# Selected attention by groups of heads: eight heads of the first token block at once, four of the second

## The reference, cut to what matters

```
q_chunk = (start + arange(128)) // 64                 # one block of 128 queries
admissible = key_chunk[None, :] <= q_chunk[:, None]
score = sum_h w[t,h] * relu(q_idx[t,h] . k_idx[s])    # the indexer
top_val, top_idx = top_k(where(admissible, score, -inf), 128)
logits = einsum('bqhd,bqkhd->bhqk', q, k[top_idx]) * 64 ** -0.5
p = softmax(where(valid, logits, -inf))
out = einsum('bhqk,bqkhd->bqhd', p, v[top_idx])
```

## Time and profile before

| what | us |
|---|---|
| median of three runs | 2717.39 |
| lowest and highest | 2716.45, 2717.55 |
| profiled execution, its own time | 2718.07 |
| its span | 2716.8 |
| TensorE busy in it | 2677.7 (99%) |
| VectorE busy | 1219.1 (45%) |
| ScalarE busy | 1049.5 (39%) |
| GpSimd busy | 1139.0 (42%) |

### The profile page before, as it was taken

One profiled execution on the slowest core, in us unless ns is written; L12 is line 12 of the kernel. 1 busy time (PEld: TensorE's weight loads), 2 busy tenths in 40 slices (PEclk: granted clock), 3 DMA queues, 4 the chain that ended last, 5 costly groups with the idle time before them and its releaser, 6 DMA issues.

```text
span 2716.8 us, 36054 instructions
## 1 busy us (share of the span) xinstructions
PE 2677.7 (99%) x13721; PEld 2153.6 (79%) x13721; DVE 1219.1 (45%) x2468; ACT 1049.5 (39%) x2005; POOL 1139.0 (42%) x894
## 2 busy tenths in 40 slices
PE   8999999999999999999999999999999999999998
PEld 6888888897778877776788888887777678888887
DVE  4434334443555456544246424265644423642426
ACT  3333434443446343452333424234445333342422
POOL 4434344435342443333365444444333336444443
PEclk9999999999999999999999999999999999999999
DMA  6444343432331332224252333324222425233331
GB/s 191 130 116 124 98 125 97 130 125 86 109 94 55 112 97 78 78 82 134 100 182 72 116 93 95 99 79 130 81 68 88 136 93 175 83 118 100 93 93 63
DMA packets 215056, 286.39 MB, mean 105 GB/s; under 512 B 16862, under 2 KB 154562, under 8 KB 214116
## 3 DMA queue, kind: packets, MB, share of 16 engines
q1 hardware_dynamic: 214884, 284.08, 34.2%
HBM read 248.31 MB, written 18.94 MB: 98 GB/s over the span
## 4 chain that ended last, share of the span: by engine, by line
PE 96%; DVE 2%; ACT 1%; POOL 1%; issue 1%; DMA 0%; ACTq 0%; DVEq 0%; POOLq 0%
PE banks L1687 39%; PE banks L1684 29%; PE banks L1680 13%; PE banks L1818 2%; PE banks L1705 2%; PE banks L1744 1%; PE banks L1800 1%; PE banks L1904 1%; PE banks L1720 1%; PE banks L1927 1%; PE banks L1839 1%; PE banks L1977 1%; PE banks L1861 1%; PE banks L1890 1%; PE banks L1786 1%; PE banks L1915 1%
## 5 line engine op out<-in xcount | busy, mean ns | idle before, releaser
L2991 POOL TENSOR_TENSOR WS<-WR,WS 128x512 fp32r<-128x512 f32 (+2 forms) x676 | 856.3, 1300 | 1048.6 <-ACT WS L2040 1048.6
L1687 PE MATMUL banks<-WS,UT 128*128 128x512 f32 (+1 forms) x3696 | 797.0, 365 | 3.9 <-DVE UT L2393 3.9
L1687 PEld LDWEIGHTS banks<-WS,UT 128*128 128x128 f32 x3696 | 605.8, 190 | 131.4 <-issue 36.4
L1684 PE MATMUL banks<-UT,WS 128*128 128x512 f32 (+1 forms) x2832 | 660.8, 392 | 0.7 <-ACT AR L2222 0.7
L1684 PEld LDWEIGHTS banks<-UT,WS 128*128 128x128 f32 (+1 forms) x2832 | 526.0, 187 | 125.8 <-issue 16.0
L2040 ACT ACTIVATE WS<-WR 128x1024 fp32r<-128x1024 f32 (+1 forms) x344 | 333.1, 1018 | 221.4 <-PE banks L1687 144.3
L1680 PE MATMUL banks<-UT,WS 128*128 128x512 f32 x1536 | 371.1, 395 | 0.0
L1680 PEld LDWEIGHTS banks<-UT,WS 128*128 128x128 f32 x1536 | 282.5, 188 | 61.9 <-issue 4.9
L1687 PE MATMUL banks<-WS,AT 128*128 128x512 f32 x1296 | 308.5, 396 | 0.0
L1687 PEld LDWEIGHTS banks<-WS,AT 128*128 128x128 f32 x1296 | 242.4, 188 | 58.2 <-ACT WS L2040 0.7
L2989 POOL TENSOR_TENSOR WS<-WR,WS 128x512 fp32r<-128x512 f32 x128 | 177.9, 1422 | 251.6 <-ACT WS L2036 251.6
(11 more groups left out here) (226 smaller groups left out, 2665.2 us busy)
## 6 DMA issues: line engine op xcount, KB each, us to landing
WR<-in_w_in SPq DMA_DIRECT2D x112, 512.0 KB, 3.6
WR<-in_w_up SPq DMA_DIRECT2D x88, 512.0 KB, 3.5
WR<-in_dil_w_in SPq DMA_DIRECT2D x64, 512.0 KB, 3.8
WR<-in_w_down SPq DMA_DIRECT2D x40, 512.0 KB, 3.7
WR<-in_diff_w_in SPq DMA_DIRECT2D x32, 512.0 KB, 3.8
WR<-in_dil_w_in SPq DMA_DIRECT2D x32, 256.0 KB, 3.2
AR<-AF SPq DMA_DIRECT2D x128, 64.0 KB, 2.3
AR<-AF SPq DMA_DIRECT2D x64, 128.0 KB, 2.4
```

What stands on the lines that cost most here:

```text
L1684: mm = pe.matmul(B[bank][0:c, :], w[part][:, kk, g * P:g * P + c], act[:, other, kk, :], start=start, stop=stop)
L1687: mm = pe.matmul(B[bank][:, off:off + n], act[:, other, before_k + kk, g * P:g * P + P], w[part][:, kk, :], start=start, stop=stop)
L2991: ge.tensor_tensor(slot(i, 1)[:, s], raw(i)[:, s], slot(i, 0)[:, s].bitcast(F32), ALU.subtract).then_inc(lo_p.sem, 1)
```

## The change

The 32 units are grouped. `att_groups()` lists (first unit, m), with m pairs of heads in each group: one group of 4 pairs for block 0, two groups of 2 pairs for block 1, and single pairs for blocks 2 and 3. One `scores3` step multiplies all m pairs, side by side in banks 4 and 5 (m w columns in each). There are two `turn3` steps, one for each half of the group's heads, each with m (b + 1) transposes into one bank and one copy by ScalarE. One `out3` makes the sums of all m pairs in one bank with one copy by VectorE. The reciprocals are taken m at a time. Each step yields as many turns as the single steps that it takes the place of: m for scores (one more for the first), m for each turn, m for the sums. Small values get places of their own, as there are now eight of each.

```diff
+def att_groups():
+    return [(0, 4), (8, 2), (12, 2)] + [(n, 1) for n in range(16, 32, 2)]
...
-                if n % 2 == 0:
-                    self.step("scores3", l, n)
+                self.step("scores3", l, n, m)
+                for _ in range(m + (n == 0)):
                     yield
-                    if n == 0:
-                        yield
-
-            def turn(n):
-                self.step("turn3", l, n)
-                yield
-
-            def out_of(n):
-                if n % 2:
-                    self.step("out3", l, n)
+
+            def turn(n, m, half):
+                self.step("turn3", l, n, m, half)
+                for _ in range(m):
                     yield
 
-            yield from self.staged(len(units), [scores, turn, out_of])
+            def out_of(n, m):
+                self.step("out3", l, n, m)
+                for _ in range(m):
+                    yield
+
+            for g in range(len(groups) + 1):
+                if g > 0:
+                    yield from turn(*groups[g - 1], 1)
+                if g < len(groups):
+                    yield from scores(*groups[g])
+                if g > 0:
+                    yield from out_of(*groups[g - 1])
+                if g < len(groups):
+                    yield from turn(*groups[g], 0)
...
# tensor()
-                    for e in range(2):
-                        r = 64 * e
-                        mm = pe.matmul(B[4 + e][:, 0:w], aqT[r:r + 64, h // 2, b * P:b * P + P],
-                                       akT[r:r + 64, h // 2, 0:w], start=True, stop=True)
+                    for q in range(m):
+                        for e in range(2):
+                            r = slice(64 * e, 64 * e + 64)
+                            mm = pe.matmul(B[4 + e][:, q * w:q * w + w], aqT[r, h // 2 + q, b * P:b * P + P],
+                                           akT[r, h // 2 + q, 0:w], start=True, stop=True)
                     mm.then_inc(scored.sem, 1)
...
-                    pe.wait_ge(weights_scaled.sem, weights_scaled.at["3", l, n])
+                    e = n + half * m + m - 1
+                    pe.wait_ge(weights_scaled.sem, weights_scaled.at["3", l, e])
...
-                    for j in range(b + 1):
-                        mm = pe.transpose(B[k][:, j * P:j * P + P], arr(o_p + 512 * e + j * P, P), IDN)
+                    for j in range(m * (b + 1)):
+                        o = o_p + 512 * half + P * j
+                        mm = pe.transpose(B[k][:, j * P:j * P + P], arr(o, P), IDN)
...
-                    for j in range(b + 1):
-                        for e in range(2):
-                            o = (h - 1 + e) * 64
-                            mm = pe.matmul(B[ob][64 * e:64 * e + 64, 0:P], av[:, j, o:o + 64],
-                                           arr(o_pt + 512 * e + j * P, P), start=(j == 0), stop=(j == b))
+                    for q in range(m):
+                        for j in range(b + 1):
+                            for e in range(2):
+                                o = (h + 2 * q + e) * 64
+                                pt = o_pt + 512 // m * (2 * q + e) + j * P
+                                mm = pe.matmul(B[ob][64 * e:64 * e + 64, P * q:P * q + P], av[:, j, o:o + 64],
+                                               arr(pt, P), start=(j == 0), stop=(j == b))
...
# scalar(), scores3 and turn3
+                    for e in range(2 * m):
+                        v = arr(o_p + 512 // m * e, w)
                         se.wait_ge(maxed.sem, maxed.at["3", l, n + e])
-                        if n >= 2:
-                            se.wait_ge(weights_scaled.sem, weights_scaled.at["3", l, n + e - 2])
+                        if e == 0 and n > 0:
+                            se.wait_ge(weights_scaled.sem, weights_scaled.at["3", l, n - 1])
...
+                    w = P * (sel_units[n][0] + 1) * m
+                    se.wait_ge(pturned.sem, pturned.at["3", l, n, half])
...
# vector(), scores3
+                    for e in range(2 * m):
+                        if n > 0 and 512 // m * e % 512 == 0:
+                            ve.wait_ge(pturned.sem, pturned.at["3", l, g, e // m])
+                        o = e // 2 * w
+                        ve.tensor_tensor_reduce(arr(o_p + 512 // m * e, w), B[4 + e % 2][:, o:o + w],
                                                 SEL[b] if b else CT[:, C_KM:C_KM + P], -0.125, -GONE, ALU.add,
-                                                ALU.min, SM[:, MX + e:MX + e + 1]).then_inc(maxed.sem, 1)
+                                                ALU.min, SM[:, MX3 + e:MX3 + e + 1]).then_inc(maxed.sem, 1)
+                    for half in range(2):
+                        z = slice(m * half, m * half + m)
+                        ve.wait_ge(exped.sem, exped.at["3", l, n + z.stop - 1])
+                        ve.reciprocal(SM[:, RZ3 + z.start:RZ3 + z.stop],
+                                      SM[:, ZS3 + z.start:ZS3 + z.stop]).then_inc(recip.sem, 1)
+                        ve.wait_ge(recip.sem, recip.at["3", l, n, half])
+                        for e in range(m * half, m * half + m):
+                            v = arr(o_p + 512 // m * e, w)
+                            ve.tensor_scalar(v, v, SM[:, RZ3 + e:RZ3 + e + 1], None,
+                                             ALU.mult).then_inc(weights_scaled.sem, 1)
...
# vector(), out3
-                    ve.tensor_copy(XA[:, h // 2, b * P:b * P + P],
-                                   B[bank6["out", "3", l, n]][:, 0:P]).then_inc(out_copied.sem, 1)
+                    ve.tensor_copy(XA[:, h // 2:h // 2 + m, b * P:b * P + P],
+                                   B[bank6["out", "3", l, n]][:, 0:P * m].rearrange("p (q t) -> p q t", q=m)
+                                   ).then_inc(out_copied.sem, 1)
```

More of the change, by code:

```diff
@@ L972, in build @@
         E32, QT, SUB, LJ = 344, 384, 512, 640
+        MX3, ZS3, RZ3 = 640, 648, 656
         oSIN, oCOS = 17088, 17120
@@ L1270, in build @@
                 key = (kind[-1], *a)
+                if kind == "turn3":
+                    l, n, m, half = a
+                    key = ("3", l, n, half)
                 k = takes_corner(("turn", *key))
@@ L1274, in build @@
             elif kind in ("out1", "out2", "out3"):
-                key = (kind[-1], *a)
+                key = ("3", *a[:2]) if kind == "out3" else (kind[-1], *a)
                 k = takes_corner(("out", *key))
@@ L1906, in tensor @@
                     mm.then_inc(scored.sem, 1)
                 elif kind == "turn3":
-                    l, n = a
-                    b, e = sel_units[n][0], n % 2
-                    pe.wait_ge(weights_scaled.sem, weights_scaled.at["3", l, n])
-                    k = bank6["turn", "3", l, n]
-                    pe.wait_ge(*before["turn", "3", l, n])
-                    for j in range(b + 1):
-                        mm = pe.transpose(B[k][:, j * P:j * P + P], arr(o_p + 512 * e + j * P, P), IDN)
+                    l, n, m, half = a
@@ L1916, in tensor @@
+                    b = sel_units[n][0]
+                    e = n + half * m + m - 1
+                    pe.wait_ge(weights_scaled.sem, weights_scaled.at["3", l, e])
+                    k = bank6["turn", "3", l, n, half]
+                    pe.wait_ge(*before["turn", "3", l, n, half])
+                    for j in range(m * (b + 1)):
+                        o = o_p + 512 * half + P * j
+                        mm = pe.transpose(B[k][:, j * P:j * P + P], arr(o, P), IDN)
                     mm.then_inc(pturned.sem, 1)
@@ L1918, in tensor @@
                 elif kind == "out3":
-                    l, n = a
+                    l, n, m = a
                     b, h = sel_units[n]
-                    pe.wait_ge(pt_out.sem, pt_out.at["3", l, n])
+                    pe.wait_ge(pt_out.sem, pt_out.at["3", l, n, 1])
                     ob = bank6["out", "3", l, n]
                     pe.wait_ge(*before["out", "3", l, n])
-                    for j in range(b + 1):
-                        for e in range(2):
-                            o = (h - 1 + e) * 64
-                            mm = pe.matmul(B[ob][64 * e:64 * e + 64, 0:P], av[:, j, o:o + 64],
-                                           arr(o_pt + 512 * e + j * P, P), start=(j == 0), stop=(j == b))
+                    for q in range(m):
[5 more added lines that the diff above has]
+                                               arr(pt, P), start=(j == 0), stop=(j == b))
@@ L2252, in scalar @@
                 elif kind == "scores3":
-                    l, n = a
+                    l, n, m = a
                     w = P * (sel_units[n][0] + 1)
-                    for e in range(2):
-                        v = arr(o_p + 512 * e, 512)[:, 0:w]
+                    for e in range(2 * m):
+                        v = arr(o_p + 512 // m * e, w)
                         se.wait_ge(maxed.sem, maxed.at["3", l, n + e])
-                        if n >= 2:
```

(24 more changed lines are left out.)

24 lines of the change are left out of this document (10 added, 14 removed).

## The result

The changed kernel takes 2710.67 us (median of 9 runs, 2709.04 to 2711.92). The kernel before takes 2717.55 (9 runs, 2716.45 to 2719.57). The ratio is 0.9973, with a 95% interval from 0.9963 to 0.9982: 6.9 us faster, with 2710.0 forecast.

A forecast was written before the change was run, and what follows sets the result against it. TensorE, 99% busy, was taken as the bound. Savings of 1.92 and 1.80 us make 3.72 a layer, 7.4 in two hybrid layers: profiled 2718.07 to 2710.7, so 2710.0 for the median; range 2708.3 to 2712.4.

The forecast's parts named there:

- What bounds the kernel: TensorE, busy 99% of the span; changes on other engines count only if they alter TensorE's time or make it wait.
- The price of a step: On TensorE, a half-array step costs its body and about 0.23 us of edges; a transpose step about 0.14 of restart.
- The bodies: Time inside grouped steps: eight-head scores 1.08 us (upper bound 1.19), four-head scores 1.07, sums of 16 records 1.03.
- rival (a): Each pass in grouped scores costs what a lone step's pass does: 0.98 us a layer less saved, 2712.0; chance 0.06.
- The sum: Selected attention saves 1.92 us in the first block and 1.80 in the second: 3.72 a layer, 7.4 in two layers.
- The waits: Before the first eight-head turn, scaled rows are ready in 4.2 to 8.7 us, inside 9.9 of cover: zero added.
- rival (b): A stall at the first eight-head turn: 6.9 us late, 13.8 in two layers, giving 2723.8 us; chance 0.03.
- Given back later: Saved time is lost at a later wait not set by TensorE (DMA weights, GpSimd's low parts): 2717.4 us; chance 0.04.

The follow-up runs named there:

- single_small: The changed kernel with single reciprocals, sums copied by pairs and transposed weights copied in m pieces, as before the change; 2710.08 us.
- same_half: The changed kernel, but each grouped scores step multiplies all its even heads first, then all the odd ones; 2711.97 us.
- The run with the cover gone: The changed kernel with no wide matmuls between the first block's eight-head scores step and its first transposes; 2720.92 us.
- singles: The changed kernel's code with all sixteen groups as single pairs, a control with TensorE's list as before the change; 2717.72 us.
- joined: The changed kernel, but the previous group's sums directly follow a group's scores with no turn between, ten joins a layer; 2706.82 us.

## Why the prediction was right

**What bounds the kernel.** Right. TensorE is at 99% in both, its list is what the time follows, and putting the small instructions of the other engines back changed nothing (single_small).

**The price of a step.** Right, and now shown by experiments that change only the number of interruptions. The edges of a half-array step were put at 0.23 us. A join that takes one pair of edges away saves 0.21 to 0.22. Grouping takes 20 of 64 steps away in a layer and 14 of 62 interruptions, because before it some steps stood together. That is worth 2.19 us. The other 1.39 are shorter bodies, so fewer interruptions are not the whole of the gain. The prediction had both in its sum, the second as bodies that grow by their columns alone.

**The bodies.** New scores step of eight heads: 1.08 forecast, 1.09 measured (1043.37 to 1044.46). The scores of the two blocks take 1.00 us less in a layer, which is what rival (a) would have lost (0.98). Four heads of 256 columns: 1.07 and 1.07 (1099.22 to 1100.29). Sums of 16 records: 1.03 and 1.03. Four transposes: 0.35 and 0.36.

**The sum.** 1.92 forecast for the first block and 1.88 measured, 1.80 and 1.74 for the second, 3.72 and 3.58 for the layer. The terms are 2 to 4% too large. They come from long stretches less hundreds of wide matmuls at 0.227 us, and the prediction had put 0.2 us a layer on that; which term was too large is not shown. Twice 3.58 is 7.2 us, and the medians differ by 6.9.

**A reason that was wrong beside a number that was right.** I chose 1.08 over 1.19 because even and odd heads take turns in the list. The choice held, but what the turns save is only the stretch in which one half runs alone, not the hiding of each load. Rival (a), each pass as dear as in a lone step, is excluded by the 1.09, and same_half shows that its ground fails too.

**The waits.** Zero was right. The chain took 3.6 us, below the 4.2 to 8.7 that were worked out: the prediction took 0.55 us for an exponential, the median of all widths, and those of 128 columns follow one another 0.39 us apart (four starts from 1044.92 to 1046.09). Four scalings took 1.27 us, near the 1.2 of the fast bound, but not for its reason: the first took 0.68 and the others start 0.20 apart. The rule of the Trainium skill on VectorE and GpSimd (SBUF — State Buffer, Who interferes with whom) agrees with that 0.68, as GpSimd was in an instruction until 1047.41. In the second layer the first scaling took 0.68 us too. That is 0.4 us out of a margin of 6.0, so it did not reach TensorE.

**What the rival of a stall left out.** I priced a late turn at its own length. The run with the cover gone shows that a wait of 3.5 us costs 5.2 to 6.3 us. With that, rival (b) decides against the change at a lateness below the 3.7 us a layer that the prediction gave: at 3.54 us the kernel is already slower than the one before (ratio 1.0014, 1.0005 to 1.0023). It did not come about, so the forecast did not suffer.

**Given back later.** It was not. The difference of the two traces is the same to 0.06 us at the decay product of the first layer and at the first scores of the second: 1205.83 less 1200.31 is 5.52, 1932.00 less 1926.54 is 5.46. It is 9.05 at the second decay product and 9.1 at the end.

## What to carry to other kernels

When one engine is at 99%, with its count of instructions fixed, ask what each interruption of its stream costs. Here leaving the full-array stream for half-array matmuls and coming back costs about 0.22 us on top of what is done inside, so small steps of the same kind are worth collecting, and those of different half-array forms are worth putting side by side. A grouped step can also be shorter than its parts together: 1.39 of the 3.58 us came from there. Before moving a step nearer to its producer, work out when its data are ready, because a wait can cost more than its length. For differences under 0.3% compare the length of the changed stretch in two traces, not their spans.

## What the runs showed of the hardware

- A stretch of 160.52 us of TensorE's work repeated to 0.01 us between two layers and two kernels (before and singles); in joined the two layers differ by 0.06. Meanwhile the medians of the kernel before moved by 0.7 us between the groups of runs (2717.08 to 2717.77) and its single runs by more than 3.
- After a wait of 3.54 us, wide matmuls ran at the 1.2 GHz level (granted clock 0.50 from 1050 to 1055 us), after which the granted clock rose again (0.92 from 1055 to 1060). After the same wait in the second layer it was 0.67 from 1940 to 1945, and 1.00 then. After a wait of 0.66 us at the same place the clock stayed at 1.00.
- A run of matmuls on one half of the array, followed by a run on the other, overlapped from the fifth matmul on: 16 records of 128 columns took 1.64 us (1043.91 to 1045.55) in place of 1.09. Eight records of 256 columns in the same order took 1.07 us (1076.41 to 1077.48), as in turn.
- The scores of one pair of heads with 128 columns took 0.42 us as a step, those of four pairs in one step 1.09, not 1.68.
- A VectorE scaling of 128 by 128 took 0.68 us in place of 0.28 where GpSimd was in an instruction as it began, in both layers of the changed kernel.
